# A two-layer diffusion trunk on one core: squares of the residual stream summed tile by tile on TensorE, and a pair of modulation columns in another bank

## The reference

```python
def _rms_norm(x, g):
    return x * lax.rsqrt(jnp.mean(x * x, axis=-1, keepdims=True) + EPS) * g
...
for i in range(DEPTH):                       # DEPTH = 2
    mod_l = jnp.split((silu(c) @ ada_w[i] + ada_b[i]), 6)      # shift, scale, gate, twice
    h = _rms_norm(x, norm_pre_mix[i]) * (1 + sc_m) + sh_m
    y = rglru_mixer(h) if i == 0 else pool_mixer(h)
    x = x + g_m * _rms_norm(y, norm_post_mix[i])
    h = _rms_norm(x, norm_pre_ffn[i]) * (1 + sc_f) + sh_f
    u, v = split(h @ w_up)
    f = (gelu(dwconv3(u)) * v) @ w_down
    x = x + g_f * _rms_norm(f, norm_post_ffn[i])
return x
```

## Time and profile before

| | |
|---|---|
| time, median of 3 runs | 2208.05 us (2205.14 to 2209.15) |
| the profiled execution | 2208.69 us, of which span 2207.2 us |
| granted clock of TensorE, mean | 0.964 of full |
| TensorE busy | 2071.9 us, 94% |
| VectorE busy | 1543.5 us, 70% |
| GpSimd busy | 1319.2 us, 60% |
| ScalarE busy | 814.3 us, 37% |
| transfers, mean | 81 GB/s |

### The profile page before, as it was taken

One profiled execution on the slowest core, in us unless ns is written; L12 is line 12 of the kernel. 1 busy time (PEld: TensorE's weight loads), 2 busy tenths in 40 slices (PEclk: granted clock), 3 DMA queues, 4 the chain that ended last, 5 costly groups with the idle time before them and its releaser, 6 DMA issues.

```text
span 2207.2 us, 26642 instructions
## 1 busy us (share of the span) xinstructions
PE 2071.9 (94%) x9056; PEld 1680.6 (76%) x9056; DVE 1543.5 (70%) x1525; ACT 814.3 (37%) x1094; POOL 1319.2 (60%) x837
## 2 busy tenths in 40 slices
PE   7899999788899999999999969799999999999996
PEld 7677776576688888888888758677888888888885
DVE  6688887768877777777777774794666555665557
ACT  3575666345222222232322335453222322223322
POOL 1433235765867787778777553457667666667653
PEclk9999999888999999999999969899999999999998
DMA  6132322422122222222222410201111111111114
GB/s 277 68 124 76 119 77 85 162 69 104 67 86 86 86 76 86 95 86 78 84 86 86 144 56 20 86 29 48 57 57 48 48 48 57 57 50 45 52 44 152
DMA packets 54330, 179.67 MB, mean 81 GB/s; under 512 B 4976, under 2 KB 6288, under 8 KB 53136
## 3 DMA queue, kind: packets, MB, share of 16 engines
q1 hardware_dynamic: 54288, 179.13, 22.9%
HBM read 166.52 MB, written 12.58 MB: 81 GB/s over the span
## 4 chain that ended last, share of the span: by engine, by line
PE 76%; DVE 9%; ACT 7%; issue 4%; POOL 3%; DMA 1%; ACTq 0%; POOLq 0%; SPq 0%; DVEq 0%
PE ps L756 38%; PE ps L491 29%; PE ps L613 3%; PE ps L878 1%; PE ps L530 1%; ACT TH L1040 1%; DVE V L1581 1%; POOL X L1325 1%; PE ps L845 1%; PE ps L556 1%; DVE Y L1673 1%; DVE T_lo L1976 1%; PE ps L866 1%; DVE Y L1660 1%; PE ps L578 1%
## 5 line engine op out<-in xcount | busy, mean ns | idle before, releaser
L1893 DVE TENSOR_TENSOR Y<-Y,ps 128x1024 f32<-128x1024 f32 x336 | 409.8, 1220 | 55.3 <-PE ps L491 15.1
L1491 POOL TENSOR_TENSOR F_lo<-S,F_hi 128x1024 fp32r<-128x1024 f32 x44 | 107.3, 2439 | 381.2 <-ACT F_hi L1169 381.2
L491 PE MATMUL ps<-F_hi,WC_hi 128*128 128x512 f32 x736 | 231.7, 393 | 7.4 <-DVE Y L1893 4.7
L1140 ACT ACTIVATE S<-S 128x1024 f32<-128x1024 f32 x48 | 50.9, 1060 | 489.4 <-DVE S L1988 489.4
L491 PE MATMUL ps<-F_hi,WC_lo 128*128 128x512 f32 x736 | 229.8, 390 | 0.0
L939 ACT ACTIVATE So_hi<-So_raw 128x512 fp32r<-128x512 f32 x132 | 82.6, 627 | 380.0 <-POOL So_raw L1343 380.0
L491 PE MATMUL ps<-F_lo,WC_hi 128*128 128x512 f32 x704 | 217.8, 391 | 0.0
L1465 POOL TENSOR_TENSOR So_lo<-So_raw,So_hi 128x512 fp32r<-128x512 f32 x132 | 189.4, 1460 | 1.5 <-ACT So_hi L939 1.5
L491 PEld LDWEIGHTS ps<-F_hi,WC_hi 128*128 128x128 f32 x736 | 138.3, 189 | 38.2 <-DVE Y L1893 5.2
L491 PEld LDWEIGHTS ps<-F_hi,WC_lo 128*128 128x128 f32 x736 | 138.6, 188 | 29.2
L2042 DVE TENSOR_TENSOR U<-t,ps 128x512 f32<-128x512 f32 x44 | 30.2, 687 | 179.2 <-PE ps L756 179.2
(11 more groups left out here) (288 smaller groups left out, 5435.3 us busy)
## 6 DMA issues: line engine op xcount, KB each, us to landing
rawA<-wA SPq DMA_DIRECT2D x64, 512.0 KB, 3.2
rawB<-wB SPq DMA_DIRECT2D x64, 512.0 KB, 3.2
E<-ada SPq DMA_DIRECT2D x47, 512.0 KB, 3.2
rawC<-wC SPq DMA_DIRECT2D x46, 512.0 KB, 4.1
quad<-ada SPq DMA_DIRECT2D x8, 2048.0 KB, 9.2
ada_first<-ada SPq DMA_DIRECT2D x4, 2048.0 KB, 16.4
outT<-X SPq DMA_DIRECT2D x16, 512.0 KB, 3.0
X<-outT SPq DMA_DIRECT2D x16, 512.0 KB, 7.2
```

The costliest lines, as they stand in the source:

```text
L491: mm = pe.matmul(out, w[:, w_cols:w_cols + P], (hi, lo)[part], start=first and w is W_hi[s] and part == 0, stop=last and w is W_lo[s])
L1140: A(S[0][:], S[0][:], ACT.Gelu_apprx_tanh).then_inc(gelu_done, 1)
L1491: TT(dst[:], S[1][:], F_hi[:].bitcast(F32), ALU.subtract).then_inc(f_ready, 1)
L1893: TT(Y[:, m], Y[:, m], flat(ps[:, b:b + 2, :]), ALU.add).then_inc(d_added, 1)
```

## The change

The sums of squares of a half now have four forms (`form`): "tree" is as before (q = 0, and half 0 of odd q), "merged" is the old form of an even q and is left for half 0 of q = 2, "open" (half 1 of odd q) gives TensorE four tiles, namely the even sum of tiles 0, 2 and 4, the odd sum of 1, 3 and 5, tile 6 and tile 7, and "direct" (half 1 of q = 2, and both halves of q = 4 and 6) gives it all eight tiles of squares. TensorE sums 64 tiles in place of 26 over the eight norms; 28 additions of 128x512 leave VectorE and 10 leave GpSimd.

The order changes with it. Behind the first FFN and the pooling mixer (`next_norms`, q = 3 and 5) the first six tiles of the next stream's half 0 are summed ahead of the spread of q's half 1. In the pooling mixer the sums of q = 4, half 1, move behind the third z tile, and their spread behind the fourth. On ScalarE the first square of the next stream comes ahead of the last square of the output, two more ahead of the root of q's half 1, and the pieces between squares move. In the first step of the first FFN the modulation columns write bank 4, without the wait for the gated product, and VectorE reduces their second half between remainders, ahead of the gated product; the down product of block 1 waits for these columns one row of tiles earlier.

The diff, with its core (the rest is the same counts of semaphores on the other engines; `odd_sum` and `even_sum` are no longer called for the direct forms):

```diff
@@ -282,12 +282,23 @@
             return (W_hi["C"][:], spare[:, 0:D], spare[:, D:2 * D])[b // 2][:, b % 2 * HF:b % 2 * HF + HF]
-        def tree(q, h):
-
-            return q == 0 or h == 0 and q in (1, 3, 5, 7)
-
-        def trees_to(q, h):
-            return sum(tree(n, h) for n in range(q + 1))
+        def form(q, h):
+
+            if q == 0 or q % 2 and h == 0:
+                return "tree"
+            if q % 2:
+                return "open"
+            return "merged" if (q, h) == (2, 0) else "direct"
+
+        def adds_to(q, h, tree, merged, opened):
+
+            return sum({"tree": tree, "merged": merged, "open": opened, "direct": 0}[form(n, h)] for n in range(q))
+
+        def evens_to(q, h):
+            return adds_to(q, h, 3, 3, 2)
+
+        def odds_to(q, h):
+            return adds_to(q, h, 2, 2, 2)
         def square_slot(q, h, p):
@@ -303,7 +314,7 @@
         def ssq_bank(q, h):
-            return 2 if q in (3, 7) else 6 + h if q == 4 else 4 + h
+            return 2 if q in (3, 7) else 6 if q == 4 else 4 + h
         def rb_bank(q, h):
@@ -532,22 +543,32 @@
                     mm.then_inc(ssq_done[h], 1)
+            def direct_sums(q, h, ps_):
+
+                for p in ps_:
+                    pe.wait_ge(sq_made[h], 8 * q + p + 1)
+                    column_sums(q, h, *square_slot(q, h, p), p == 0, p == KT - 1)
+
             def square_sums(q, h):
                 last, total = square_slot(q, h, KT - 1), square_slot(q, h, 0)
-                if tree(q, h):
-                    pe.wait_ge(sum_last[h], trees_to(q, h))
+                kind = form(q, h)
+                if kind == "tree":
+                    pe.wait_ge(sum_last[h], adds_to(q, h, 1, 0, 0) + 1)
                     column_sums(q, h, *total, True, True)
-                elif q % 2:
-                    pe.wait_ge(sum_both[h], q + 1)
+                elif kind == "open":
+                    pe.wait_ge(sum_even[h], evens_to(q, h) + 2)
                     column_sums(q, h, *total, True, False)
-                    pe.wait_ge(sq_made[h], 8 * q + 8)
-                    column_sums(q, h, *last, False, True)
-                else:
+                    pe.wait_ge(sum_odd[h], odds_to(q, h) + 2)
+                    column_sums(q, h, *square_slot(q, h, 1), False, False)
+                    direct_sums(q, h, (KT - 2, KT - 1))
+                elif kind == "merged":
                     pe.wait_ge(sq_made[h], 8 * q + 8)
                     column_sums(q, h, *last, True, False)
-                    pe.wait_ge(sum_both[h], q + 1)
+                    pe.wait_ge(sum_both[h], adds_to(q, h, 1, 1, 0) + 1)
                     column_sums(q, h, *total, False, True)
+                else:
+                    direct_sums(q, h, range(KT))
             def spread(q, h):
@@ -561,6 +582,14 @@
                 spread(q, h)
+
+            def next_norms(q):
+
+                square_sums(q, 1)
+                direct_sums(q + 1, 0, range(6))
+                spread(q, 1)
+                direct_sums(q + 1, 0, (6, 7))
+                spread(q + 1, 0)
             pe.wait_ge(memset_done, 3)
@@ -693,7 +722,7 @@
                         pe.wait_ge(d_added, 8 * c)
-                        if m == 1 and L == 0:
+                        if m == (not (isinstance(j, int) and j == 1)) and L == 0:
                             pe.wait_ge(ada_added, NH + 2 + j)
@@ -769,10 +800,8 @@
                 if L == 0:
-                    if first:
-                        pe.wait_ge(f_mul, 2)
                     pe.wait_ge(ada_added, NH + j)
-                    ada_columns(4 * NH + 2 * j, 2, ps[:, 0, 0:2])
+                    ada_columns(4 * NH + 2 * j, 2, ps[:, 4 if first else 0, 0:2])
                 quarter("S4", t, first)
@@ -808,7 +837,7 @@
                 for h in range(2):
-                    if L or h:
+                    if h:
                         norm(2 + 4 * L, h)
@@ -881,12 +909,12 @@
                 mm.then_inc(pool_mm, 1)
-            for i in range(2):
+            for i in range(3):
                 z_tile(i)
+            pe.wait_ge(x_scaled, 40)
             square_sums(4, 1)
-            z_tile(2)
+            z_tile(3)
             spread(4, 1)
-            z_tile(3)
             for i in range(4, KT):
@@ -1086,15 +1113,18 @@
             def next_stream(q, i, fill):
-                squares_x(q + 1, i, 0, range(KT))
+                squares_x(q + 1, i, 0, (1, 2))
+                norm_root(q, 1)
+                squares_x(q + 1, i, 0, range(3, KT))
                 norm_root(q + 1, 0)
                 squares_x(q + 1, i, 1, range(4))
-                if fill is not None:
-                    fill(0)
-                squares_x(q + 1, i, 1, range(4, KT))
+                fill(0)
+                squares_x(q + 1, i, 1, (4, 5))
+                if q == 3:
+                    z_hi(0)
+                squares_x(q + 1, i, 1, (6, 7))
                 norm_root(q + 1, 1)
-                if fill is not None:
-                    fill(1)
+                fill(1)
             def fill_ffn(L, h, ks=range(KT)):
@@ -1230,11 +1260,14 @@
                 for n in range(2 * KT):
+                    if n == 2 * KT - 1 and L == 0:
+                        squares_x(q + 1, 1, 0, (0,))
                     act.wait_ge(d_added, 8 * (FJ * (L + 1) - 2) + n + 1)
                         norm_root(q, 0)
-                norm_root(q, 1)
+                if L:
+                    norm_root(q, 1)
             ffn(0)
@@ -1683,30 +1708,19 @@
             def last_gates(q, i):
-                even_sum(q, 1, 6)
-                merge_sums(q, 1)
                 gate_tiles(i, q, 0, (4, 5))
             def next_stream(q, i, fill, late=None):
-                even_sum(q + 1, 0, 2)
-                even_sum(q + 1, 0, 4)
                 if q == 5:
                 gate_tiles(i, q, 1, (0, 1))
-                even_sum(q + 1, 0, 6)
-                merge_sums(q + 1, 0)
+                norm_scale(q + 1, 0)
                 gate_tiles(i, q, 1, (2, 3))
-                norm_scale(q + 1, 0)
                 scale_tiles(i + 1, q + 1, 0, X, fill)
-                gate_tiles(i, q, 1, (4, 5))
-                even_sum(q + 1, 1, 2)
-                gate_tiles(i, q, 1, (6, 7))
-                even_sum(q + 1, 1, 4)
-                even_sum(q + 1, 1, 6)
-                merge_sums(q + 1, 1)
+                gate_tiles(i, q, 1, range(4, KT))
                 if late:
@@ -2029,14 +2038,14 @@
                     conv_right(L, j - 1)
-                if L == 0:
+                if L == 0 and not first:
                     ada_sum(j - 1, 1)
                 if L == 0:
-                    add_ada_bias(ps[:, 0, 0:2], 46 + 2 * j, 2, NH + 1 + j)
+                    add_ada_bias(ps[:, 4 if first else 0, 0:2], 46 + 2 * j, 2, NH + 1 + j)
                     ada_sum(j, 0)
```

More of the change, by code:

```diff
@@ L741, in down_last @@
                         spread(q, 0)
-                square_sums(q, 1)
-                spread(q, 1)
+                if L == 0:
+                    next_norms(q)
+                else:
+                    norm(q, 1)
             def quarter(name, t, first=False):
@@ L830, in _ @@
             ffn(0)
-            norm(4, 0)
             def z_tile(i):
@@ L897, in _ @@
                     spread(5, 0)
-            square_sums(5, 1)
-            spread(5, 1)
+            next_norms(5)
             ffn(1)
@@ L1256, in pool_start @@
                 else:
-                    for i in range(3):
+                    for i in (1, 2):
                         z_hi(i)
@@ L1269, in _ @@
                 h, mt = n // KT, BOX_TILES[n]
+                if n == 2 * KT - 1:
+                    squares_x(6, 2, 0, (0,))
                 act.wait_ge(pool_evac, n + 1)
@@ L1298, in odd_sum @@
                 if p > 3:
-                    pool.wait_ge(sum_odd[h], 2 * q + p // 2 - 1)
+                    pool.wait_ge(sum_odd[h], odds_to(q, h) + p // 2 - 1)
                 to = square_cols(q, h, 1)
@@ L1584, in merge_sums @@
                 total, odd = square_cols(q, h, 0), square_cols(q, h, 1)
-                dve.wait_ge(sum_even[h], 3 * q + 3)
-                dve.wait_ge(sum_odd[h], 2 * q + 2)
+                dve.wait_ge(sum_even[h], evens_to(q, h) + 3)
+                dve.wait_ge(sum_odd[h], odds_to(q, h) + 2)
                 TT(total, total, odd, ALU.add).then_inc(sum_both[h], 1)
-                if tree(q, h):
-                    dve.wait_ge(sum_both[h], q + 1)
+                if form(q, h) == "tree":
+                    dve.wait_ge(sum_both[h], adds_to(q, h, 1, 1, 0) + 1)
                     dve.wait_ge(sq_made[h], 8 * q + 8)
@@ L2020, in ffn_first @@
                 right_lo(L, 0)
+                if L == 0:
+                    ada_sum(1, 1)
                 right_lo(L, 1)
```

29 lines of the change are left out of this document (6 added, 23 removed).

## The result

The changed kernel takes 2222.66 us (median of 4 runs, 2219.29 to 2226.50), the kernel before 2208.6 us beside it: 1.0067 times as long, 95% interval 1.0046 to 1.0088. It is slower by 14 us; 9 had been forecast. The profiled execution took 2226.5 us, span 2225.0, 17.8 us more than the profiled one before.

A forecast was written before the change was run, and what follows sets the result against it. TensorE was taken as the bound, idle only between stages, with narrow sums falling to half clock. Terms -0.9 - 5.4 + 10.0 + 8.7 - 3.0 = +9.4 us on the 2208.05 us median gave 2217 us, range 2196 to 2228.

The forecast's parts named there:

- Rival 1: TensorE's clock stays full through the narrow sums: -20.9 us, 2187 us; chance 0.10.
- rival 2: Narrow matmuls do not raise the clock but hold it where full: about -10 us, 2198 us; chance 0.09.
- rival 4: Wide work around the sums closes up, so they cost half as much in B and C: 2208 us; chance 0.07.
- Rival 3: The gain of S is given back as TensorE waits on GpSimd's chain in the next steps: 2223 us; chance 0.08.
- A: First block, squares of output and residual, second half (q 1 and 2): -0.9 us (-4.5 to +2.6).
- S: First pipelined step of the first FFN, modulation columns no longer waiting for the gated product: -5.4 us (-4.7 to -6.3).
- B: End of the first FFN to the pooling mixer (q 3 and 4): +10.0 us (-4.5 to +13.7).
- C: Pooling mixer to second FFN (q 5 and 6): +8.7 us (-2.8 to +12.2).
- D: End of the program (q 7), last tile's sum and tail of gates: -3.0 us (-2.6 to -3.8).
- the price of an eight-tile block: Eight-tile sum right behind wide matmuls: 4.2 us at full clock, then 5.9 at half, 10.1 us in all.
- the new wait: In S, TensorE waits for ScalarE's copy of t1 in place of the gated product: 3.9 us of 8.5.

The follow-up runs named there:

- seven: The changed kernel with two idle 128-wide matmuls behind each of the first seven tiles of the q 2, 4, 6, half 1 sums: 2233.76 us.
- eight: The changed kernel with eight idle 128-wide matmuls behind each of the first seven tiles of the q 2, 4, 6, half 1 sums: 2243.66 us, single run.
- old_place: The changed kernel with the q 4, half 1 sums back behind the second z tile and their spread behind the third: 2216.93 us.
- open_outputs: The kernel before with only the four-tile sums of the second halves of q 1, 3, 5 and 7: 2199.94 us, ratio 0.9962.

## Why the prediction was right, and where it missed

**The mechanism held.** Narrow matmuls begin at what is left of the full clock and go on at half: 64 in a row, 0.112 us apart and then 0.213. The start of the program, on which I had leaned, shows half clock by its spacing alone; the profile's clock column reads 1.00 for 15.73 to 29.38 us. The new blocks bear the spacing out, since they have 0.213 us where that column reads 0.50. Rival 1 (clock full) and rival 2 (narrow matmuls hold it) are refuted by that and by seven and eight; rival 4 (half hidden) by the blocks' starting right behind the wide products and the scaling that waits for them. Rival 3's 2223 us is nearer to the measured 2222.66 than my 2217, but its mechanism did not come: between 570 and 640 us TensorE waited only for t1 (3.5 us) and for VectorE's addition in the first step's own down product (0.50 us), not for GpSimd, and the stage kept 3.9 us.

**The sum** of the stages missed by 4.9 us (+14.3 without the start, +9.4 forecast): A 0.5, S 1.5, B 0.2, C 2.9, D -0.2.

**A** -0.9 forecast, -0.4 measured (q 1 gained 2.7 us instead of 1.9, the block behind it cost 1.3 more). **D** -3.0 and -3.2.

**B** +10.0 and +10.2, and this agreement is luck. Scaling of half 0 came at 1302.94, where 1303.0 is the forecast less the 0.8 us by which TensorE was early. Scaling of half 1, for which the +10.0 was worked out, came at 1337.57 where 1326.63 less 0.8 would be no change, so 11.7 us late:

```profile
1337.57 5.36 DVE L1685 SCALAR_TENSOR_TENSOR Y<-X,cA,ps 128x512 f32<-128x512 f32 x8 [4.83 <-PE ps L577]
```

The block took 0.9 us more than its price, and most of the rest is the fourth z tile. Then 1.5 us came back, 1.4 of them in the window sums, where the clock of the kernel before had fallen and that of the changed one had not (0.72 against 1.00, shown below the stage table).

**The step that failed is the price of an eight-tile block**: "10.1" us, from a mean of 4.2 us of full clock behind the last wide matmul. The blocks took 11.4, 11.0 and 11.6 us. The seven stretches from which I had the 4.2 were mostly idle; beginning with narrow work gave no more, and in this execution less (2.3 to 3.0 us). That makes 3.7 us over three blocks. Stage C's 2.9 us are 1.5 of that, 0.7 ahead of the block (it began 4.3 us late against the stage's start, 3.6 forecast) and the rest in the products behind it. Part of this is chance: over nine blocks the mean was 10.7 us, and old_place shows that C can also be 8.5. In a run whose blocks took that mean the forecast would have been 1.9 us nearer.

**S** was mis-sized by 1.5 us: -5.4 forecast, -3.9 measured. I had the new wait (3.48 us against "3.9"). But I let the clock be full again 4 us into the three quarters, and it was half for 6 of them (589.1 to 595.1), which cost 0.7 us; at the start of the down product the gain was 4.7. Then 0.8 us of it went in the down product, 0.50 of them in the wait for VectorE's addition, which I had not looked at.

**The start** (+3.5 us in this profile) was in no term: the same code takes 0 to 4 us more or less from run to run. It builds up where the granted clock differs (1.00 and 0.57 in the first of the two stretches shown; 0.89 and 0.86 over 340 to 475 us). Why the clock falls there in one execution and not in the other is open.

## What to carry to other kernels

Before work moves to an engine that waits, ask at what clock it will run there, and whether it comes during the wait or behind it: one tile summed as the last square arrives gained some 3 us a stage, eight in series took 9 to 12 us where two had taken 4 to 5 with their waits. A wait in which TensorE stands idle can be worth filling with wide work whose result nobody reads, sized from the wait in the trace and kept short of it: here that gave 4 to 7 us in its second form, and nothing clear of noise in its first. And a part that gains can hide in a change that loses: of this change's four parts the output sums gained 8 to 9 us and the first step probably 3, while the eight-tile sums of first halves with the new order cost 4 to 6 and those of second halves some 20.

## What the hardware showed beyond this

A remainder of 128x512 took 0.68 us on VectorE by itself and mostly 1.74 to 1.79 us beside GpSimd's, whose own then took 1.71 to 1.77 but for the first. In one profile of thirteen (open_outputs) GpSimd's took 4.89 us while VectorE's ran at 0.68, and the modulation columns of the first FFN's first step came 6 us earlier, though the step itself was only 1.5 us shorter. What decides which engine yields is not shown.
